# The sample attention and the last output projection of a decoder step become one stage

## What is computed

```python
def sb_block(q_blk, q_start, k, v, bias):
    z = jnp.einsum('bqhd,bkhd->bhqk', q_blk, k) + bias[None, :, None, None]
    lneg = jnp.where(valid, jax.nn.log_sigmoid(-z), 0.0)
    suffix = lax.cumsum(lneg, axis=3, reverse=True) - lneg
    w = jnp.where(valid, jnp.exp(jax.nn.log_sigmoid(z) + suffix), 0.0)
    return jnp.einsum('bhqk,bkhd->bqhd', w, v)
...
            o = sb_attention(q, keys, vals, b_sb[i], pos0).reshape(Bn, T, SB_WIDTH) * jax.nn.silu(gate)
            h = h + o.astype(h.dtype) @ w_out_b[i]
    return rmsnorm(h, g_final), jnp.stack(new_s), k_sh, v_sh
```

## Time and profile before

| | us |
|---|---|
| median of 3 runs | 3666.59 (3665.02 to 3667.06) |
| the profiled execution | 3668.44 |
| its span | 3666.8 |
| PE busy | 3335.9 (91%) |
| DVE busy | 1649.4 (45%) |
| ACT busy | 1445.9 (39%) |
| mean granted PE clock | 0.953 |

### The profile page before, as it was taken

One profiled execution on the slowest core, in us unless ns is written; L12 is line 12 of the kernel. 1 busy time (PEld: TensorE's weight loads), 2 busy tenths in 40 slices (PEclk: granted clock), 3 DMA queues, 4 the chain that ended last, 5 costly groups with the idle time before them and its releaser, 6 DMA issues. The chain is left out here.

```text
span 3666.8 us, 50175 instructions
## 1 busy us (share of the span) xinstructions
PE 3335.9 (91%) x17844; PEld 2414.5 (66%) x17844; DVE 1649.4 (45%) x1964; ACT 1445.9 (39%) x2341; POOL 757.5 (21%) x807
## 2 busy tenths in 40 slices
PE   7999997877779799999999799999999996888798
PEld 6999997443458699999999344444444443444487
DVE  5111111777633331111110588788888884333333
ACT  5111111665421121111111588787878883223321
POOL 0000000000001100000000467666666762000000
PEclk9999998888889899999999799999999998999999
DMA  4222212333154432222221632323232203999843
GB/s 140 70 69 69 69 59 78 106 117 117 66 185 160 144 128 69 69 69 70 69 69 46 180 91 86 99 58 98 81 96 61 64 18 123 375 371 370 327 145 106
DMA packets 240021, 439.20 MB, mean 120 GB/s; under 512 B 24821, under 2 KB 148538, under 8 KB 227802
## 3 DMA queue, kind: packets, MB, share of 16 engines
q1 hardware_dynamic: 224714, 351.87, 29.1%
q0 software_dynamic: 15152, 85.34, 6.5%
HBM read 313.03 MB, written 124.13 MB: 119 GB/s over the span
## 5 line engine op out<-in xcount | busy, mean ns | idle before, releaser
L1603 POOL TENSOR_TENSOR att_w<-att_w,att_rest 128x1023 f32<-128x1023 f32 (+7 forms) x384 | 613.4, 1599 | 337.6 <-DVE att_rest L1568 333.9
L416 PE MATMUL projb_acc<-projb_x_hi,projb_w_hi 128*128 128x416 f32 x1280 | 452.4, 353 | 26.3 <-DVE projb_x_lo L407 26.3
L416 PE MATMUL projb_acc<-projb_x_hi,projb_w_lo 128*128 128x416 f32 x1280 | 450.1, 352 | 0.0
L416 PE MATMUL projb_acc<-projb_x_lo,projb_w_hi 128*128 128x416 f32 x1280 | 449.7, 351 | 0.0
L1469 PE MATMUL att_z<-att_k,att_q 64*128 64x512 f32 (+3 forms) x1280 | 401.9, 587 | 2.7 <-ACT att_w L1520 2.7
L1512 ACT ACTIVATE att_rest<-att_z,att_bias 128x1024 f32<-128x1024 f32 (+7 forms) x384 | 332.8, 867 | 110.7 <-PE att_z L1469 86.0
L1433 PEld LDWEIGHTS att_wT_acc<-const_ident,att_w 128*128 128x128 f32 x2176 | 232.6, 141 | 216.5 <-issue 122.2
L1568 DVE TENSOR_TENSOR_SCAN att_rest<-att_rest,att_zero 128x128 f32<-128x128 f32 (+7 forms) x256 | 358.6, 1406 | 26.1 <-ACT att_rest L1512 25.3
L274 PE MATMUL proja_acc<-proja_x_hi,proja_w_hi 128*128 128x416 f32 x1000 | 353.3, 353 | 0.8 <-DVE proja_x_lo L247 0.7
L274 PE MATMUL proja_acc<-proja_x_hi,proja_w_lo 128*128 128x416 f32 x1000 | 351.5, 352 | 0.0
L274 PE MATMUL proja_acc<-proja_x_lo,proja_w_hi 128*128 128x416 f32 x1000 | 349.7, 350 | 0.0
(11 more groups left out here) (224 smaller groups left out, 4674.0 us busy)
## 6 DMA issues: line engine op xcount, KB each, us to landing
smp_k_pages<-in_cache_k SPq DMA_DIRECT2D x128, 512.0 KB, 9.1
smp_v_pages<-in_cache_v SPq DMA_DIRECT2D x128, 512.0 KB, 10.1
proj_b<-projb_out POOLq DMA_DIRECT2D x32, 1040.0 KB, 4.6
proj_a<-proja_out POOLq DMA_DIRECT2D x24, 1040.0 KB, 4.5
att_q<-proj_b SPq DMA_DIRECT2D x64, 256.0 KB, 4.1
att_k<-proj_b SPq DMA_DIRECT2D x14, 1024.0 KB, 13.3
proja_w_raw<-in_w_in_a SPq DMA_DIRECT2D x24, 512.0 KB, 4.0
gla_vgT<-proj_a SPq DMA_DIRECT2D x24, 512.0 KB, 6.1
```

Of the source, the lines that this page charges most:

```text
L416: mm = pe.matmul(acc[:, q, 0:size], w[:, b, k, :], x[:, k, at:at + size], start=(k == 0 and w is w_hi and x is x_hi), stop=(k == KD - 1 an ...
L1603: pool.tensor_tensor(these, these, passed[:, 1:size], ALU.mult).then_inc(w_made, 1)
```

## The change

The two stages become one function, `sample_attention_and_out`. The main block's steps n = 1 to 4 of the four pairs are 16, and each carries the products of one tile of 128 prompt tokens (tile 4q + n - 1); the tile of the sample tokens follows behind the loop, taken from SBUF. After each two value pages PE turns the halves of two key pages one by one, and three products of the tile stand behind each half. The key slots in PSUM are three half pages instead of two pages; turned keys have one buffer instead of two, and the rings of pages are 6 and 6 instead of 10 and 12. SP loads the pages in the order in which PE uses them. POOL stores the result of a tile, then loads the residual of the next tile into the one buffer `h`, and then the `oT` tile after that. The projection's weights are loaded and split in the first block, in the place of the turned keys. The y sums of a tile use one bank, one column half after the other. The square of the norm goes into `y`. Samples' weights have two buffers of 512 instead of one of the whole length.

```diff
-def sample_attention(nc, c, projT, b_sb, cache_k, cache_v, page_table, k_out, v_out, oT):
+def sample_attention_and_out(nc, c, projT, b_sb, cache_k, cache_v, page_table, k_out, v_out, oT, w_out, residual, gain,
+                             y_out):
...
-    k_ring, v_ring = 10, 12
+    k_ring, v_ring, turn_ring = 6, 6, 3
     per_group = 8
     per_pair = per_group * groups
-    all_pages, ahead = per_pair * n_pairs, 2 * per_group
+    all_pages = per_pair * n_pairs
...
-        kT = s.sb("kT", [P, 2, 2, blocks, BANK])
-        w = s.sb("w", [P, past + P])
-        pass_on = s.sb("pass_on", [P, 2, BANK])
+        kT = s.sb("kT", [P, 2, blocks, BANK])
+        w_old, w_new = s.sb("w_old", [P, 2, BANK]), s.sb("w_new", [P, P])
...
-        kT_ps = s.ps("kT_acc", [P, 2, D])
+        w_hi, w_lo = (s.sb(n, [P, KD, D], F32R) for n in ("w_hi", "w_lo"))
+        oT_lo, oT_hi = (s.sb(n, [P, 2, KD, P], F32R) for n in ("oT_lo", "oT_hi"))
+        h, y, gains = s.sb("h", [P, D]), s.sb("y", [P, D]), s.sb("gains", [P, D])
+        eps, sumsq, root, rstd = (s.sb(n, [P, 1]) for n in ("eps", "sumsq", "root", "rstd"))
+        kT_ps = s.ps("kT_acc", [P, turn_ring, BANK])
...
+        y_ps = s.ps("y_acc", [P, BANK])
...
+        def load_oT(engine, t):
+            engine.dma_start(oT_lo[:, t % 2, :, :].bitcast(F32), oT.rearrange("(k p) n -> p k n", p=P)
+                             [:, :, t * P:(t + 1) * P]).then_inc(oT_in[t % 2], 16)
+
+        w_raw = kT[:, :, :, :].rearrange("p s b n -> p (s b n)").rearrange("p (k n) -> p k n", n=D)
+        new_k = rest[0:SMP, 0:D]
...
+                for k in range(KD):
+                    sp.dma_start(w_raw[:, k, :], w_out[k * P:(k + 1) * P, :]).then_inc(w_in[k], 16)
...
+                for n in range(v_ring):
+                    load_values(sp, n)
...
+                for t in range(2):
+                    load_oT(pool, t)
+                pool.dma_start(gains[:, :], gain.unsqueeze(0).broadcast_to([P, D])).then_inc(gain_in, 16)
+                pool.dma_start(h[:, :], residual(0)).then_inc(res_in, 16)
...
+                for k in range(KD):
+                    dve.wait_ge(w_hi_made, k + 1)
+                    dve.tensor_tensor(w_lo[:, k, :], w_raw[:, k, :], w_hi[:, k, :].bitcast(F32),
+                                      ALU.subtract).then_inc(w_lo_made, 1)
+                dve.wait_ge(w_lo_made, KD)
...
+        def turned_in(q, n, p):
+
+            g = groups * q + n + 1
+            if n == groups or g >= groups * n_pairs:
+                return ()
+            return (per_group * g + 2 * p, per_group * g + 2 * p + 1)
...
+        def tile_of(q, n):
+
+            return groups * q + n - 1
...
-            for n in range(k_ring, all_pages + ahead):
-                if n < all_pages:
-                    load_keys(sp, n)
-                if n >= ahead:
-                    load_values(sp, n - ahead)
-            sp.wait_ge(gated, n_pairs)
-            sp.dma_start(oT.rearrange("(b p) n -> p b n", p=P)[:, :, SEQ:TOK], out[:, :, :]).then_inc(out_stored, 16)
-            sp.wait_ge(out_stored, 16)
+            pages = [("k", m) for m in range(per_group)]
+            for q in range(n_pairs):
+                for n in range(n_w):
+                    for p in range(4):
+                        pages += [("k", m) for m in turned_in(q, n, p)]
+                        if n > 0:
+                            first = q * per_pair + (n - 1) * per_group + 2 * p
+                            pages += [("v", first), ("v", first + 1)]
+            for kind, m in pages:
+                if kind == "k" and m >= k_ring:
+                    load_keys(sp, m)
+                elif kind == "v" and m >= v_ring:
+                    load_values(sp, m)
+
+        @block.gpsimd
+        def _(pool):
+            for t in range(n_tiles):
+                n = rows_of(t)
+                pool.wait_ge(normed, t + 1)
+                pool.wait_ge(gain_in, 16)
+                pool.dma_start(y_out(t), y[0:n, :]).then_inc(y_stored, 16)
+                if t + 1 < n_tiles:
+                    pool.dma_start(h[0:rows_of(t + 1), :], residual(t + 1)).then_inc(res_in, 16)
+                if t + 2 < NT:
+                    pool.wait_ge(y_made, 2 * t + 2)
+                    load_oT(pool, t + 2)
+            pool.wait_ge(y_stored, 16 * n_tiles)
...
-            def turn_keys(n):
-                pe.wait_ge(k_in[n % k_ring], 16 * (n // k_ring + 1))
-                if n >= 2:
-                    pe.wait_ge(act_copied, n - 1)
-                    pe.wait_ge(dve_copied, n - 1)
-                for hp in range(blocks):
-                    mm = pe.transpose(kT_ps[:, n % 2, hp * P:(hp + 1) * P],
+            def turn_half(n, e):
+                u = 2 * n + e
+                if e == 0:
+                    pe.wait_ge(k_in[n % k_ring], 16 * (n // k_ring + 1))
+                if u >= turn_ring:
+                    was = u - turn_ring
+                    pe.wait_ge(dve_copied if was % 2 else act_copied, was // 2 + 1)
+                for j in range(4):
+                    hp = half * e + j
+                    mm = pe.transpose(kT_ps[:, u % turn_ring, j * P:(j + 1) * P],
                                       k_pages[:, n % k_ring, hp * P:(hp + 1) * P], c.ident[:, :])
                 mm.then_inc(k_turned, 1)
...
+            def out_products(t, j, k0, k1):
+                if k0 == 0:
+                    if j == 0:
+                        pe.wait_ge(lo_made, t + 1)
+                    if j or t:
+                        pe.wait_ge(h_made, 2 * t + j)
+                for k in range(k0, k1):
+                    for x, wt in ((oT_hi, w_hi), (oT_hi, w_lo), (oT_lo, w_hi)):
+                        mm = pe.matmul(y_ps[:, :], x[:, t % 2, k, :], wt[:, k, j * BANK:(j + 1) * BANK],
+                                       start=(k == 0 and x is oT_hi and wt is w_hi), stop=(k == KD - 1 and x is oT_lo))
+                if k1 == KD:
+                    mm.then_inc(y_made, 1)
...
-                    g = groups * q + n + 1
                     for p in range(4):
-                        if n < groups and g < groups * n_pairs:
-                            turn_keys(per_group * g + 2 * p)
-                            turn_keys(per_group * g + 2 * p + 1)
+                        halves = [(m, e) for m in turned_in(q, n, p) for e in range(2)]
                         if n > 0 or p == 0:
                             values(q, n, p)
+                        for i in range(4):
+                            if halves:
+                                turn_half(*halves[i])
+                            if n > 0:
+                                out_products(tile_of(q, n), p // 2, p % 2 * 4 + i, p % 2 * 4 + i + 1)
             fold(n_pairs - 1)
+            for j in range(2):
+                out_products(NT, j, 0, KD)
...
+                if m == 0 and g >= 1:
+                    act.wait_ge(z_made, logits_of(g - 1))
+                act.activation(kT[:, m % 2, 0:half, m // 2 * P:(m // 2 + 1) * P],
+                               kT_ps[:, 2 * n % turn_ring, :].rearrange("p (h n) -> p h n", n=P),
...
+            def high_part(t):
+                n = rows_of(t)
+                if t >= 2:
+                    act.wait_ge(y_made, 2 * t - 2)
+                if t < NT:
+                    act.wait_ge(oT_in[t % 2], 16 * (t // 2 + 1))
+                    src = oT_lo[:, t % 2, :, :].bitcast(F32)
+                else:
+                    act.wait_ge(gated, n_pairs)
+                    src = out[:, :, :]
+                act.activation(oT_hi[:, t % 2, :, 0:n], src, ACT.Copy).then_inc(hi_made, 1)
+
+            def norm(t):
+                n = rows_of(t)
+                act.wait_ge(h_made, 2 * t + 2)
+                if t >= 1:
+                    act.wait_ge(y_stored, 16 * t)
+                    act.wait_ge(rstd_made, t)
+                act.activation(y[0:n, :], h[0:n, :], ACT.Square, accum_out=sumsq[0:n, :]).then_inc(sumsq_made, 1)
+                act.wait_ge(sumsq_made, t + 1)
+                act.activation(root[0:n, :], sumsq[0:n, :], ACT.Sqrt, scale=1.0 / D, bias=eps[0:n, :]).then_inc(root_made, 1)
...
             sigmoid(0, 0)
+            high_part(0)
             for q in range(n_pairs):
                 for n in range(n_w):
                     copy_weights(q, n)
+                    t = tile_of(q, n)
+                    if t >= 1 and n > 0:
+                        norm(t - 1)
                     if n + 1 < n_w:
                         sigmoid(q, n + 1)
                     elif q + 1 < n_pairs:
                         sigmoid(q + 1, 0)
-                    g = groups * q + n + 1
-                    if n < groups and g < groups * n_pairs:
-                        for m in range(per_group):
-                            copy_keys(per_group * g + m)
+                    if n > 0 and t + 1 < NT:
+                        high_part(t + 1)
+                    for p in range(4):
+                        for m in turned_in(q, n, p):
```

(87 more changed lines are left out.)

90 lines of the change are left out of this document (47 added, 43 removed).

## The result

The changed kernel takes 3798.23 us (median of 4 runs, 3795.65 to 3802.69), the kernel before 3666.82 us beside it: 1.036 of it, 95% interval 1.0347 to 1.0373. The profiled execution has a span of 3799.0 us, 132.2 more. The direction was forecast, the size was not: 3698 us, with a range that ended at 3737.

What follows compares the result with a forecast made beforehand. The loop was taken as mostly DMA transfer, the last projection's products as TensorE-bound. Merging without new waits gave 3583 us; ten waits of 9.4 + 2.2 us added 116: 3699 us span, forecast 3698, range 3650 to 3737.

Steps and rivals of the forecast that it cites:

- loop to end without waits: Merged loop of 453 us, bound by TensorE, then 14.7 us for the sample tile, before any new wait is added.
- first block: Setup ahead of the loop: SP's extra weight loads and value pages, less four key pages, make it 6.5 us longer.
- ten waits for key copies: TensorE stands 9.4 us in each of ten key-turning steps, as key copies queue behind ACT's high part, awaiting its load.
- waits for the residual add: Not foreseen: in a pair's last step TensorE's own 16 us of work was to cover the late load.
- low clock behind the waits: After each of the ten waits TensorE runs four to five us at half speed, losing some 2.2 us.
- The mechanism: In ten steps ACT's high part and the key copies behind it wait for a load issued only after the previous tile's finish.
- The landing: Load of the heads' output in a step: issued at 11.5 us, landed 4.9 us later, at 16.4.
- Mixing products and transposes: In the loop, 16 switches a step cost some 0.07 us each: 12 us in all, between nothing and 40 us.
- The rings: In the loop, six pages of each kind, 15 us of transfer, cost nothing; too small rings added nothing to the forecast.
- The drain: The skill's 1.38 us per table switch, left out; it would add 28 us over ten steps, making 3726 us.
- The late case: Rival: loop transfers shared half and half, waits of 12.8 + 2.5 us a step, 3751 us; chance 0.13, from 3735 on.
- upper bound of 12.8 us for a wait: Longest TensorE wait per step, if store, residual and heads' output share the DMA engines half and half with pages.

Runs made afterwards that it cites:

- e7: e6 with the first block's order of e5 and the heads' output loaded as early as in e3: 3592.8 us, 0.9797 of the kernel before.
- e2: Merged kernel with DVE adding the residual's first half ahead of the next tile's low part, in a pair's last step (n = 4) only: 3783.2 us.
- e1: Merged kernel with key copies (and DVE's first residual add) ahead of the next tile's high and low parts: 3706.9 us.
- e3: Merged kernel with POOL's load of the heads' output issued once its buffer is free, no longer behind finish, store and residual load: 3672.3 us.
- e5: Merged kernel with SP's first-block order changed: biases ahead of the weights, masks among them, new keys and values ahead of the pages: 3786.0 us.
- e8: e7 with page rings of 4 and 4 instead of 6 and 5: 3663.6 us, 0.9987 of the kernel before.
- e4: Merged kernel with Square in place of Sqrt in the norm, leaving the root out of its results and the function table switch with it: 3774.7 us.
- e6: e1 with two residual buffers instead of one, loaded two tiles ahead, and a value ring of 5 pages: 3626.1 us.

## Why the prediction was wrong, and where it was right

The table accounts for the 100 us between the forecast span (3699) and the measured one (3799.0), term by term, in us. e7 stands for the merged stage without the waits, and the last row is what is left over, so the sum closes by construction:

| term | forecast | measured | off by |
|---|---|---|---|
| loop to end without waits | 476.5 | 482.4 (e7: 3108.6 to 3591.0) | 6 |
| first block | 6.5 more | 20.5 more | 14 |
| ten waits for key copies | 94 | 112.1 | 18 |
| waits for the residual add | 0 | 58.3 (61.1, less 2.8 in e7) | 58 |
| low clock behind the waits | 22 | 26 (what is left between the merged kernel and e7) | 4 |

- **The step that failed** is the sentence "In the last step of a pair no copy stands behind the high part, and 16 us of TensorE's own work cover it." I had looked only at what stands behind the high part on ACT. On DVE the residual add stands behind the low part, and half of TensorE's work in that step stands behind the add. The rule of the code was in the text ("DVE: ... low part of T+1, then its key copies"), the add after the second group of copies was left out of it. In its place the runs showed four waits of 12.4 to 14.3 us, 54.7 in all, and steps of 33.1 us (3250.10 to 3283.19) where 16 were forecast. They showed more than that: e2 took the low part away in three of the four and won a quarter of what I expected, since the residual's load, issued in the same place, keeps TensorE waiting for 9 us by itself. Its wait is the second term that the prediction put at nothing.
- **The mechanism was right**, by e1 and e3: the load is issued 10.7 us into the step (forecast 11.5), and moving its issue, or moving the copies ahead of it, takes the ten waits away. The 10 steps were the right ones; seven of the waits were 10.1 to 10.6 us and those in step n = 1 of each later pair 12.6 to 13.8.
- **The landing was mis-sized.** 4.9 us was taken from the earlier trace rows; here it was 6.5 in a plain step, 10.1 in step n = 1 of the second pair (issued at 3307.95, used at 3318.09) and 12.9 in a last step. That is most of the 18 us of the table's third row. The row that 4.9 came from was of a stage with a DMA share of 0.39. The forecast's "once TensorE stops, the rings fill and the pages leave the engines free" came nearer in the plain steps than where SP had several pages to fetch, six in the last step.
- **The first block was mis-sized** because I added up SP's issue time and not what queues in front of the small loads. e5 gives 12 of the 14 us back.
- **The clock** cost what was forecast for each wait. e7's plain steps, at a granted clock of 1.00, are 26.8 us from one turning of the weights to the next:

```profile
3301.23 0.60 PE L1901 MATMUL smp_wT_acc<-const_ident,smp_w_old 128*128 128x128 f32 x4
...
3328.05 0.60 PE L1901 MATMUL smp_wT_acc<-const_ident,smp_w_old 128*128 128x128 f32 x4
```

With this and its wait taken off, each of the merged kernel's seven plain steps has 1.5 to 2.7 us left, 2.2 in the mean (the one shown above: 39.8 less 26.8 less 10.2). Over all waits it is some 33 us (an estimate by the same subtraction, step by step). The 26 of the table is less because e7 has some 7 us of its own, in step n = 1 of the later pairs, where value pages are late (such a step takes 28.9 to 29.7 us). No run held the clock.
- **Mixing products and transposes** was charged at 12 us and cost next to nothing: in the merged kernel a group of values, four halves and twelve products lasts 5.69 us (3149.01 to 3154.70), and its parts are 5.61 by the forecast's own rows (1.00 + 1.90 + 12 x 0.226).
- **The rings** were rightly left out of the sum, as the merged kernel's waits show; that "the smaller rings cost nothing as long as TensorE is the later one" is refuted by e8.
- **The drain** that the Trainium skill ("ScalarE: Activation LUTs", "What ACT_TABLE_LOAD costs") adds to a table switch, 1.38 us, isn't there: the load starts 0.02 us behind the root (3175.24 and 0.30 us, then 3175.56), and the sigmoid 0.01 us behind the load. The trace differs from the page, and the measurement decides. e4's 24 us call for no drain either, but can't exclude one, since the loads stand partly beside the logits.
- The late case had 0.13, and its price, 3751, was still 47 us short. All cases shared the same blind spot, so the range did too.
- Two slips in the working moved nothing. "69 products" of useful work between the stages are 22 by the earlier trace rows. And the upper bound of 12.8 us for a wait comes out at 13.3 from the terms beside it (9.4 and three times 1.29).

The merge itself pays once the new waits are gone: 84 us were forecast for it without them, and e7 has 76 (3668.4 to 3592.8), with e5's order of the first block in it.

## What to carry to other kernels

When two stages are woven into one, walk through each engine's queue in each kind of step, and for every instruction that may wait for a transfer list everything behind it, on every engine that copies its result onward. A load belongs where its buffer comes free, not where the code of its tile stands: here one issue moved was worth 126 us in the merged kernel, and still 26 where everything else had been put right. And after each wait that is taken away, ask what lands next; behind the heads' output the residual was late here, and only with both out of the way did the merge pay.

## What the runs showed that I had not expected

- A transfer of 512 KB issued by POOL landed 3.0 us after its issue in the last projection of the kernel before (the result's stores). Within the merged loop, where POOL issues three in a row, the medians were 4.6 us for the store, 7.3 for the residual and 8.4 for the heads' output. In e6's loop, at a DMA share of 0.87, the heads' output took 12 us. The merged kernel's rows:

```profile
out_y_prompt<-smp_y POOLq DMA_DIRECT2D x14, 512.0 KB, 4.6
smp_h<-h_mid POOLq DMA_DIRECT2D x14, 512.0 KB, 7.3
smp_oT_lo<-oT POOLq DMA_DIRECT2D x14, 512.0 KB, 8.4
```

- Three products in reduced float32 between groups of four float32 transposes lost 0.02 us a switch (0.08 in a group of four), though a product's weight load takes 0.188 us.
- Rings that are deep enough by their bytes (8 pages, 10 us) lost 71 us against eleven pages, which left PE 1.2 us of waits for pages in the loop (6.7 us by its weight loads).
